# Causal attention of the second block: query tiles taken in the order 0, 7, 1, 6, 2, 5, 3, 4 within a head pair, output divided for tiles t and 7-t together

## What is computed

```python
def fox_attention(q, k, v, log_f):
    scale = HEAD_DIM ** -0.5
    c = jnp.cumsum(log_f, axis=1)
    ...
    def block(args):                     # one block of 128 queries
        idx, qi, ci = args
        logits = jnp.einsum('bqhd,bkhd->bhqk', qi, k) * scale
        logits = logits + ci[..., :, None] - c_k[..., None, :]
        causal = k_pos[None, :] <= q_pos[:, None]
        logits = jnp.where(causal, logits, -jnp.inf)
        p = jax.nn.softmax(logits, axis=-1)
        return jnp.einsum('bhqk,bkhd->bqhd', p.astype(v.dtype), v)
    ...
    h = h + (o * jax.nn.silu(gate)) @ w_out_a[i]
```

## Time and profile before

| | us |
|---|---|
| median of 3 runs (2718.75 to 2720.46) | 2720.03 |
| span of the profiled execution, first to last instruction | 2712.1 |
| TensorE busy in it | 2528.4 (93%) |
| VectorE / ScalarE / GpSimd busy | 1620.0 / 1360.6 / 402.8 |
| `phase_fox`, from its first product to the end of its last instruction | 1863.08 to 2152.90 |
| mean granted TensorE clock, share of 2.4 GHz | 0.969 |

### The profile page before, as it was taken

The page is one execution under the profiler, slowest core; times in us unless marked ns, Lnnn a source line. Parts: engine busy times, 40 slices in busy tenths (PEclk is TensorE's granted clock), DMA queues, the critical chain, the costliest instruction groups (busy, mean ns, idle before and its releaser), DMA issues. The chain is left out here.

```text
span 2712.1 us, 38443 instructions
## 1 busy us (share of the span) xinstructions
PE 2528.4 (93%) x13642; PEld 2012.0 (74%) x13654; DVE 1620.0 (60%) x2941; ACT 1360.6 (50%) x2392; POOL 402.8 (15%) x558
## 2 busy tenths in 40 slices
PE   4999999999968999999977999998999899998989
PEld 4788489788847888888855878885666688886667
DVE  6662455687558999999947055412555446742751
ACT  4243244697247888888846133323555423322750
POOL 0121021331103111111102000001222200000320
PEclk7999999999989999999988999998999999999999
DMA  6642000002049999999966111043010222114201
GB/s 239 190 137 66 0 1 1 1 12 106 11 187 404 419 416 411 417 410 413 417 237 223 47 39 64 24 140 123 30 60 32 81 95 74 32 51 152 79 13 51
DMA packets 126958, 400.28 MB, mean 148 GB/s; under 512 B 11975, under 2 KB 62284, under 8 KB 114398
## 3 DMA queue, kind: packets, MB, share of 16 engines
q1 hardware_dynamic: 113370, 353.30, 34.2%
q0 software_dynamic: 12048, 42.56, 3.9%
q10 hardware_dynamic: 1396, 2.50, 0.3%
HBM read 347.93 MB, written 50.40 MB: 147 GB/s over the span
## 5 line engine op out<-in xcount | busy, mean ns | idle before, releaser
L2982 DVE CUSTOM_DVE_ANT_0 fox_l<-PS,fox_c 128x256 f32<-128x256 f32 (+7 forms) x128 | 92.0, 756 | 128.7 <-PE PS L3029 83.7
L2919 ACT ACTIVATE fox_l<-fox_l,stat 128x256 f32<-128x256 f32 (+7 forms) x128 | 98.4, 770 | 79.9 <-DVE stat L2982 79.9
L447 PE MATMUL PS<-wehd,aTh 128*128 128x512 f32 x256 | 100.7, 393 | 6.6 <-DVE aTl L2417 6.6
L447 PE MATMUL PS<-wehg,xsTh 128*128 128x512 f32 x256 | 100.8, 394 | 3.4 <-ACT xsTh L2341 2.0
L447 PE MATMUL PS<-wqkh,uTh 128*128 128x512 f32 x256 | 103.1, 403 | 0.0
L447 PE MATMUL PS<-wehu,xsTh 128*128 128x512 f32 x256 | 102.9, 402 | 0.0
L449 PE MATMUL PS<-wehg,xsTl 128*128 128x512 f32 x256 | 100.7, 393 | 0.0
L449 PE MATMUL PS<-wqkh,uTl 128*128 128x512 f32 x256 | 100.5, 392 | 0.0
L449 PE MATMUL PS<-wehd,aTl 128*128 128x512 f32 x256 | 100.4, 392 | 0.0
L449 PE MATMUL PS<-wehu,xsTl 128*128 128x512 f32 x256 | 100.1, 391 | 0.0
L448 PE MATMUL PS<-wqk_rest,uTh 128*128 128x512 f32 x256 | 100.0, 391 | 0.0
(11 more groups left out here) (600 smaller groups left out, 7502.3 us busy)
## 6 DMA issues: line engine op xcount, KB each, us to landing
we0g<-in_w_expert_gate SPq DMA_DIRECT2D x16, 2048.0 KB, 11.1
we0u<-in_w_expert_up SPq DMA_DIRECT2D x16, 2048.0 KB
we1g<-in_w_expert_gate SPq DMA_DIRECT2D x16, 2048.0 KB, 11.4
we1u<-in_w_expert_up SPq DMA_DIRECT2D x16, 2048.0 KB
we0d<-in_w_expert_down SPq DMA_DIRECT2D x16, 2048.0 KB
we1d<-in_w_expert_down SPq DMA_DIRECT2D x16, 2048.0 KB
wada_rest<-in_w_ada SPq DMA_DIRECT2D x16, 1024.0 KB, 5.9
X<-in_x SPq DMA_DIRECT2D x16, 512.0 KB, 11.7
```

The lines of the kernel that those rows point to most:

```text
L447: nc.tensor.matmul(out, lh, rh, start=start, stop=False)
L2919: nc.scalar.activation(prob(p, e)[:, 0:K], prob(p, e)[:, 0:K], ACT.Exp, bias=nbm[:, u % 8:u % 8 + 1], scale=-1.0, accum_out=rsum[:, u % 16 ...
L2982: nc.vector.tensor_tensor_reduce(out=prob(p, e)[:, 0:K], in0=PS[:, 2 * e:2 * e + 2, :].rearrange("p a b -> p (a b)")[:, 0:K], in1=C[:, h % ...
```

## The change

The tiles of a pair are no longer taken in rising size. `ORDER` gives the tile of each of the eight positions, and every place that derived the tile from p % 8 asks `tile_of(p)`. The counts of chunks are summed over `ORDER`. The division, which handles an odd position and the one before it, now covers two tiles that don't lie side by side in `qa`, `G_a`, `oh_a` and `qa_rest` (t and 7-t), so these operands are of the form 128 x 2 x 128 with a step between the two. What is computed for each tile is the same, with the same number of instructions on each engine.

```diff
+    ORDER = (0, 7, 1, 6, 2, 5, 3, 4)
+    def tile_of(p):
+        return ORDER[p % T]
     def chunks_before(p):
-        return p // T * 24 + (2 * (p % T) if p % T < 4 else 8 + 4 * (p % T - 4))
+        return p // T * 24 + sum(4 if t >= 4 else 2 for t in ORDER[:p % T])
     def second_before(p):
-        return p // T * 8 + 2 * max(0, p % T - 4)
+        return p // T * 8 + sum(2 for t in ORDER[:p % T] if t >= 4)
     def two(x, w):
-        at = (w % T - 1) * P
-        return x[:, w // T, at:at + 2 * P]
+        a, b = ORDER[w % T - 1], ORDER[w % T]
+        return x[:, w // T, :].rearrange("p (t q) -> p t q", q=P)[:, a:b + 1:b - a, :]
+    def both(x):
+        return x.rearrange("p (t q) -> p t q", q=P)
...
-                    rb = env.pad[w // 2 % 2][:, 0:2 * P]
+                    rb = both(env.pad[w // 2 % 2][:, 0:2 * P])
...
-                    nc.vector.tensor_copy(rb, PS[:, 7, 2 * P:4 * P]).then_inc(rb_out, 1)
+                    nc.vector.tensor_copy(rb, both(PS[:, 7, 2 * P:4 * P])).then_inc(rb_out, 1)
...
-                    nc.vector.tensor_tensor(two(env.qa, w), PS[:, 7, 0:2 * P], rb, ALU.mult).then_inc(o_out, 1)
+                    nc.vector.tensor_tensor(two(env.qa, w), both(PS[:, 7, 0:2 * P]), rb, ALU.mult).then_inc(o_out, 1)
...
-                if 0 <= v < NPAIR and v % T >= 4:
+                if 0 <= v < NPAIR and tile_of(v) >= 4:
...
-                    c, t = p // T, p % T
+                    c, t = p // T, tile_of(p)
```

More of the change, by code:

```diff
@@ L2872, in chunks_before @@
     def chunks_before(p):
-        return p // T * 24 + (2 * (p % T) if p % T < 4 else 8 + 4 * (p % T - 4))
+        return p // T * 24 + sum(4 if t >= 4 else 2 for t in ORDER[:p % T])
     def second_before(p):
-        return p // T * 8 + 2 * max(0, p % T - 4)
+        return p // T * 8 + sum(2 for t in ORDER[:p % T] if t >= 4)
     def two(x, w):
-        at = (w % T - 1) * P
-        return x[:, w // T, at:at + 2 * P]
-    chunk_list = [(p, half, e) for p in range(NPAIR) for half in range(2 if p % T >= 4 else 1) for e in range(2)]
+        a, b = ORDER[w % T - 1], ORDER[w % T]
+        return x[:, w // T, :].rearrange("p (t q) -> p t q", q=P)[:, a:b + 1:b - a, :]
+    def both(x):
+        return x.rearrange("p (t q) -> p t q", q=P)
+    chunk_list = [(p, half, e) for p in range(NPAIR) for half in range(2 if tile_of(p) >= 4 else 1) for e in range(2)]
     with nc.Block() as block:
@@ L2905, in _ @@
                 if 0 <= v < NPAIR:
-                    nk = min(v % T + 1, 4)
+                    nk = min(tile_of(v) + 1, 4)
                     for e in range(2):
@@ L2914, in _ @@
                 if p < NPAIR:
-                    K = (p % T + 1) * P
+                    K = (tile_of(p) + 1) * P
                     for e in range(2):
@@ L2956, in _ @@
                         dve.wait_ge(o_out, w // 2 - 1)
-                    nc.vector.tensor_copy(rb, PS[:, 7, 2 * P:4 * P]).then_inc(rb_out, 1)
+                    nc.vector.tensor_copy(rb, both(PS[:, 7, 2 * P:4 * P])).then_inc(rb_out, 1)
                     dve.wait_ge(rb_out, w // 2 + 1)
-                    nc.vector.tensor_tensor(two(env.qa, w), PS[:, 7, 0:2 * P], rb, ALU.mult).then_inc(o_out, 1)
+                    nc.vector.tensor_tensor(two(env.qa, w), both(PS[:, 7, 0:2 * P]), rb, ALU.mult).then_inc(o_out, 1)
                 v = p - LAG - 1
-                if 0 <= v < NPAIR and v % T >= 4:
-                    nk = v % T + 1 - 4
+                if 0 <= v < NPAIR and tile_of(v) >= 4:
+                    nk = tile_of(v) + 1 - 4
                     for e in range(2):
@@ L3004, in transposes @@
                             pe.wait_ge(pt_first, 2 * q + f + 1)
-                    for k in range(4 * half, min(v % T + 1, 4 * half + 4)):
+                    for k in range(4 * half, min(tile_of(v) + 1, 4 * half + 4)):
                         last = nc.tensor.transpose(PS[:, 4 + at % NTB, (k % 4) * P:(k % 4 + 1) * P],
@@ L3034, in _ @@
                 if 0 <= w < NPAIR:
-                    c, t = w // T, w % T
+                    c, t = w // T, tile_of(w)
                     pe.wait_ge(rx_ready, w + 1)
```

## The result

| | before | after |
|---|---|---|
| median, first comparison (4 runs each) | 2719.39 | 2697.90 (2697.29 to 2702.65) |
| median, five further rounds (9 and 5 runs) | 2718.27 | 2699.43 (2696.64 to 2700.17) |
| span of the profiled execution | 2712.1 | 2696.2 |
| `phase_fox`, first mask product to the end of the last GpSimd instruction | 289.82 | 270.87 |

The ratio is 0.9932 (0.9920 to 0.9944) in the first comparison and 0.9933 (0.9919 to 0.9946) in the second: about 18.5 us faster. The medians alone are 21.5 us apart in the first comparison and 18.8 in the second.

A forecast was written before the change was run, and what follows sets the result against it. TensorE is busy nearly everywhere, so only its idle time in `phase_fox` can be won: -2.4 + 13.5 - 0.1 + 5.6 = 16.6 us, span 2695.5, plus 7.9 around it 2703.4. Forecast 2699 to 2708, range 2699 to 2712.

The forecast's parts named there:

- TensorE's need: TensorE's time for a pair without any wait: 108 blocks at 0.217 us plus 0.88 fixed per step, 30.5 us.
- (b): Kernel before, n = 5, 6, 7: next logits wait for VectorE's take-out; delay 0.9 us a pair, which goes.
- (a): Kernel before, n = 8: take-outs and division precede the second-half copy a transpose chunk needs; delay 1.7 us, which goes.
- (c): Kernel before, n = 1, 2, 3: steps measured longer than their 12, 15 and 15 blocks need; delay 1.2 us.
- The pair, 32.0: A steady-state pair of the changed kernel takes 32.0 us, 2.25 less than 34.24; bounds 30.5 and 33.3.
- the places with k = 1 and k = 3: Second-half chunks of 1 and 3 blocks, whose copy waits delay TensorE by 0.48 and by 0.33 or 0.39 us.
- The start, -2.4: First pair, partly at half clock: position 9 comes at 1903.6 instead of 1901.2, a loss of 2.4 us.
- The tail, +5.6: After the last logits: 16.3 us instead of 21.93, 40 blocks remaining instead of 52; gain 5.6, bounds 2.6 and 6.5.
- The first: Rival: second-half copies come later, 0.3 us worse at four places; pair 33.2, gain 9.4, time 2711; chance 0.16.
- The third: Rival: remaining waits eat nearly all, each place 0.6 worse and start 5 us late; 2715 to 2720; chance 0.03.
- the fourth: Rival: better, with waits below the sum and the clock up early; 2694 to 2699 us; chance 0.06.
- The second: Rival: gaps in the first pair keep TensorE at half clock; a whole further pair gives 2727, slower; chance 0.04.

The follow-up runs named there:

- the added instruction: One unused 128x256 VectorE instruction between the two take-outs of n = 5 to 8, in the kernel before (2741.90 us) and in the changed kernel (2706.69 us).
- large_first: Changed kernel with order 7, 0, 6, 1, 5, 2, 4, 3, large tiles at even positions, bank 7's halves exchanged: pair 34.02 us, time 2710.55 us.
- second_half_first_old: Kernel before (rising order) with second-half transposes of p-3 ahead of the values of p-4 in TensorE's list: pair 34.23 us, time 2717.79 us.
- filled_start: Changed kernel plus unused 128x512 products in TensorE's idle times at the phase's start: position 9 at 36.19 us, phase 267.24, time 2700.07 us.
- rising_first_pair: Changed kernel with the first head pair in rising order: position 9 at 38.14 us, phase 272.99, time 2700.25 us.
- rising_last_pair: Changed kernel with the last of eight head pairs in rising order: tail 21.94 us, time 2696.72 us.

## Why the prediction was right, and by how much it was off

**TensorE's need, and where the waits stood: right.** The need of 30.5 us for a pair was never reached as a whole (31.34 is the shortest pair), but steps of 16 and 18 blocks take 4.34 and 4.77 where it says 4.35 and 4.79. All three kinds of delay were shown. (b) The take-outs: the added instruction came through in full at n = 5, 6 and 7 before, and not at all at n = 6 and 5 after. (a) Division ahead of the copy: large_first keeps the alternation and brings this back, and nearly the whole gain is gone. That is more than the prediction had given it: of 3.8 us of waits it had 1.7 to the division at n = 8 and 0.9 to the take-outs, as if the two gains were separate. The run shows that shorter large steps alone leave 0.2 us, because the small steps take up what they save if the copy comes late. (c) is of two kinds. At n = 2 the division stands ahead of the copy as well; at n = 1 and 3 it does not, and the waits there are those between a chunk and its copy, which second_half_first_old took away.

**The pair, 32.0: measured 31.74.** The terms of the prediction add up to 32.08 (30.5 + 1.5 + 0.1), which it rounded down. Predicted steps 4.8, 3.2, 4.3, 3.5, 4.8, 3.9, 4.3 and 3.2; measured 4.77, 3.07, 4.34, 3.46, 4.79, 3.75, 4.35 and 3.21. The two that were off are n = 2 and n = 4, the places with k = 1 and k = 3. Over six pairs that makes 15.05 us instead of 13.5, the largest part of what was missing. At n = 2 it was the predicted wait for the division (0.1), which is not in the trace: L3049 stands 0.84 us after the mask product of n = 2 (1971.96), just behind its logits. At n = 4 it was the wait for the copy: by the prediction's blocks it is 0.27 where it had 0.39. Why it had too much there, while the other three places come out within 0.04, is open.

**The start, -2.4: measured -1.7 (39.82 against 38.11).** The predicted mask products of the first positions (6.6, 2.4, 5.9 us apart) are 6.52, 1.82 and 5.87. The step of n = 2 ran at full clock in part. The prediction had named an early clock as a possibility worth 2.4 us; it rose for 3.4 us only and gave 0.6. The clock's part in the start was shown by filled_start. As the lag at position 9 the term was near, as a loss to the phase it is not one: rising_first_pair shows that a start in rising order ends 2.1 us later.

**The tail, +5.6: measured 5.45 (16.48 against 21.93).** Right in size. Its bound of 2.6 us by blocks is what rising_last_pair gives as the true saving of an alternating last pair (2.44). The sum of the prediction isn't touched by this, since its terms begin and end at the same mask products before and after.

**The sum, 16.6: measured 18.95 in the two traces** (-1.7 + 15.05 + 0.15 + 5.45), and about 18.5 by the ratios.

**From span to time: a wrong reading, and a good deal of luck.** The 7.9 us "around the span" were the difference of a median and a span of another execution. In every profiled run since, time and span lie 1.8 us apart (2698.02 and 2696.2). So the profiled execution of before was one of some 2714 us, an estimate from these two numbers, and times of that kernel lie between 2712.45 and 2720.46 in the runs here. The forecast was not hurt by it, since 2695.5 + 7.9 is also the median of before less the gain, 2720.03 - 16.6. That the predicted span of 2695.5 is only 0.7 us from the measured 2696.2 is luck: the phase gained 2.35 us more than the sum, and the stretches around it, where nothing was changed, were 3.05 us longer in that execution. The median of 2697.90 is 5.5 us under the forecast. Of these, 2.35 are missing in the sum, 0.64 are the kernel before (2719.39 and not 2720.03), and some 2.5 lie in none of its terms, in how executions differ. By the ratio, 0.9932 of 2720.03 is 2701.5, inside the range.

**Rivals.** The first (copies later) did not come: in steady state brackets for the copies are 0.3 at most. The third (2715 to 2720) did not come either. The first median, 2697.90, lies where the fourth had it (2694 to 2699, chance 0.06), and both of its conditions came in part: waits 0.3 us a pair below the sum, and a clock that was up early for 3.4 us. The second (the clock) is real and was only not reached: the clock fell in the changed kernel's start behind an idle time of 2.47 us, and in the order of before when its idle time was 1.98 in the place of 1.52. A whole pair at half clock would by the prediction's own 22.7 us lie at 2726, not 2727. The Trainium skill, "TensorE: Matmul & The Clock Gate", "A second HAM failure mode: psum-queue depth-cycling", describes a TensorE whose clock falls and rises again and again because it idles briefly and often between groups of products. The changed kernel's trace does not agree: four waits of 0.2 to 0.5 us in each pair leave the granted clock at 1.00 over 193.61 us. The run with the added instruction in the order of before does show a clock that falls and rises, at 1.7 us a pair beyond its 4d, but behind one idle time of 1.98 us a pair with three shorter ones ahead of it.

## What to carry to other kernels

In a software pipeline whose tiles differ in size, count for each step the work of all the stages that fall into it, and lay the large take-out beside the most work of TensorE. But look first at which iteration a step that comes once in two tiles falls into: standing ahead of a copy that frees a bank, 0.8 us of division cost 2.3 of the 2.5 us a pair that the better order gives. For a first and a last tile, compare kernels at points where the same amount of work remains, since a shorter tail may only have been paid earlier.

And take what lies around the span from a time and a span of the same execution. A forecast of a time is best written as the median before less the gain, since the stretches outside the change differ by some us from one execution to the next.

## What the runs showed of the hardware that I had not expected

TensorE's clock is sensitive to idle times that look harmless. With 1.52 us idle once in 34 us it stayed at 2.4 GHz over six pairs; with 1.98 us in the same place, and 0.5 to 0.7 us in each of the three steps ahead, it fell to 1.2 GHz in six cases of eight, and the transposes after it took 1.7 times as long for some 3 us. At a phase's start it rose under 4 us of logits, fell again behind 2.47 us of idle time, and stayed up when unused products filled part of that time. Filling the idle times of the start was worth 3.6 us of the phase, more than the exchange in TensorE's list for three of the tiles (0.4 us a pair).
